# Weighing the six expert rows of a token on TensorE in pairs, with the rows of a pair stacked on the two partition halves

## The reference

```python
scores = jax.nn.sigmoid((x2 @ w_router).astype(jnp.float32))
_, idx = lax.top_k(scores + router_bias.astype(jnp.float32), TOP_K)     # TOP_K = 6
gate = jnp.take_along_axis(scores, idx, axis=1)
gate = gate / jnp.sum(gate, axis=-1, keepdims=True) * ROUTED_SCALE
...
yb = (jax.nn.silu(xb @ w_gate[eb]) * (xb @ w_up[eb])) @ w_down[eb]      # one block of an expert's tokens
acc = acc.at[tok_b].add(yb * gate_b[:, None])                            # six weighted rows per token
shared = (jax.nn.silu(x2 @ w_sh_gate) * (x2 @ w_sh_up)) @ w_sh_down
...
x = layer_norm(DEEPNORM_ALPHA * x + acc[:T] + shared, ln2_g[i], ln2_b[i])
```

## Time and profile before

| what | us |
|---|---|
| median of three runs | 2006.47 |
| the profiled execution's own time | 1997.47 |
| its span, first to last instruction | 1995.7 |
| busy: PE / DVE / ACT / POOL | 1804.0 / 800.1 / 381.5 / 375.5 |
| Combination of layer 0, first L974 to last L1026 | 900.48 to 951.74 |
| Combination of layer 1, first L974 to last L1026 | 1940.14 to 1991.40 |

### The profile page before, as it was taken

The page is one execution under the profiler, slowest core; times in us unless marked ns, Lnnn a source line. Parts: engine busy times, 40 slices in busy tenths (PEclk is TensorE's granted clock), DMA queues, the critical chain, the costliest instruction groups (busy, mean ns, idle before and its releaser), DMA issues. The chain is left out here.

```text
span 1995.7 us, 35283 instructions
## 1 busy us (share of the span) xinstructions
PE 1804.0 (90%) x12176; PEld 1112.1 (56%) x12177; DVE 800.1 (40%) x2156; ACT 381.5 (19%) x874; POOL 375.5 (19%) x499
## 2 busy tenths in 40 slices
PE   9999999889999989879899869999789999997787
PEld 7888445446666545544344428754456666664443
DVE  4222753623333222226276763415523333332236
ACT  2111741001111111101244533211001111110020
POOL 8452000011111111110013752200011111111110
PEclk9999999989999999999899968999899999999999
DMA  6220224599999999997122120107699999999987
GB/s 232 84 70 17 96 113 191 206 401 414 420 420 421 420 421 420 421 416 296 58 70 74 41 53 3 54 33 283 279 419 394 424 421 423 421 423 423 423 364 295
DMA packets 144053, 541.75 MB, mean 271 GB/s; under 512 B 30902, under 2 KB 68370, under 8 KB 94174
## 3 DMA queue, kind: packets, MB, share of 16 engines
q1 hardware_dynamic: 122654, 490.20, 61.3%
q0 software_dynamic: 21312, 50.37, 6.5%
HBM read 521.58 MB, written 46.14 MB: 284 GB/s over the span
## 5 line engine op out<-in xcount | busy, mean ns | idle before, releaser
L669 PE MATMUL bank<-W,XT 128*64 128x256 f32 x2880 | 335.5, 390 | 43.0 <-DMA W<-in_w_exp_gate_dram 15.8
L669 PEld LDWEIGHTS bank<-W,XT 128*64 128x64 f32 x2880 | 235.6, 141 | 154.7 <-issue 39.9
L704 PE MATMUL bank<-W,ht 128*64 128x512 f32 x720 | 168.0, 608 | 13.8 <-DMA W<-in_w_exp_down_dram 8.3
L2113 PE MATMUL bank<-XT,room 128*128 128x512 f32 x352 | 157.7, 603 | 0.0
L680 DVE TENSOR_TENSOR sig<-sig,bank 128x256 f32<-128x256 f32 x72 | 30.3, 421 | 274.7 <-ACT sig L676 264.4
L722 POOL DMA_INDIRECT y_rows<-y,row x36 | 36.7, 1020 | 430.6 <-DVE y L715 430.6
L682 DVE TENSOR_TENSOR h<-sig,bank 128x256 f32<-128x256 f32 x72 | 30.4, 422 | 209.9 <-PE bank L669 209.8
L2113 PEld LDWEIGHTS bank<-XT,room 128*128 128x128 f32 x352 | 66.8, 193 | 84.5 <-issue 84.1
L722 POOL DMA_INDIRECT y_rows<-XT,row x36 | 36.4, 1010 | 407.1 <-DVE XT L715 407.1
L655 ACT ACTIVATE XT<-bank 128x512 f32<-128x512 f32 x74 | 44.2, 597 | 330.5 <-PE bank L647 330.5
L669 PE MATMUL bank<-room,XT 128*64 128x256 f32 x864 | 98.7, 380 | 8.5 <-DMA room<-in_w_exp_gate_dram 8.0
(11 more groups left out here) (457 smaller groups left out, 2746.8 us busy)
## 6 DMA issues: line engine op xcount, KB each, us to landing
W<-in_w_exp_gate_dram SPq DMA_DIRECT2D x88, 1024.0 KB
W<-in_w_exp_up_dram SPq DMA_DIRECT2D x88, 1024.0 KB
W<-in_w_exp_down_dram SPq DMA_DIRECT2D x88, 1024.0 KB
room<-in_w_exp_gate_dram SPq DMA_DIRECT2D x40, 1024.0 KB
third_high<-in_w_exp_up_dram SPq DMA_DIRECT2D x40, 1024.0 KB
third_high<-in_w_exp_down_dram SPq DMA_DIRECT2D x40, 1024.0 KB
W<-y_rows SPq DMA_DIRECT2D x8, 2048.0 KB, 14.2
room<-in_rwkv_w_in_dram SPq DMA_DIRECT2D x22, 512.0 KB
```

The costliest lines, as they stand in the source:

```text
L669: last = pe.matmul((gate, up)[m][64 * a:64 * a + 64, :], xt[s][:, k, 64 * a:64 * a + 64], weights(w, a, m)[:, k * FE:(k + 1) * FE], start= ...
L704: last = pe.matmul(B[5 + half][64 * a:64 * a + 64, :], ht[:, j, 64 * a:64 * a + 64], weights(w, a, 2)[:, at:at + 512], start=(j == 0), sto ...
L2113: last = pe.matmul(main(i)[:], wc[i % WBUFS][:, kb, :], K.XT[:, kb, :], start=(kb == 0), stop=(kb == KD - 1))
```

## The change

All six rows of a token are weighed on PE, two by two. The two rows of a pair (row numbers 2q and 2q + 1) are loaded onto the two partition halves: row 2q of 64 tokens on partitions 0 to 63, row 2q + 1 of the same tokens on 64 to 127; the tile's other 64 tokens lie behind them on the same partitions (index h). The weight is 128 x 64: two diagonals of 64 x 64 on top of each other, with the gates of the two rows. One product with it gives the weighted sum of both rows for 64 tokens, and its result goes to output partitions 64h to 64h + 63.

For the diagonals the gates must lie on the halves in the same way; four small products with the identity put them there in the first pass of the expert loop, into bank 3, and ACT copies them out. The second pass's `turn_h`, which writes bank 3, waits for that copy. DVE loses L959. Per layer there are 24 DMAs of 512 KB instead of four of 2 MB and four of 1 MB, and each pair of rows has a semaphore of its own, for which PE waits.

```diff
-BY_VECTOR = 2
-BY_TENSOR = TOPK - BY_VECTOR
+ROW_PAIRS = TOPK // 2
+HP = P // 2
+BY_VECTOR = ()
+BY_TENSOR = [(t, q) for t in range(NT) for q in range(ROW_PAIRS) if (t, q) not in BY_VECTOR]
...
         def turn_h(pe, n):
             pe.wait_ge(hidden_done, n + 1)
+            if isinstance(n, int) and n == 1:
+                pe.wait_ge(ending.gates_kept, 1)
...
+        def turn_gates(pe):
+            for h in range(2):
+                for j in range(2):
+                    last = pe.matmul(gates_bank[HP * j:HP * j + HP, h], ident[:, HP * h:HP * h + HP],
+                                     K.gates[:, :, j:TOPK:2], start=True, stop=True)
+            last.then_inc(gates_turned, 1)
+
+        def keep_gates(act):
+            act.wait_ge(gates_turned, 1)
+            act.activation(turned_gates[:], gates_bank, ACT.Copy).then_inc(ending.gates_kept, 1)
...
                     if early and n == 0:
                         from_slot(0)
+                        turn_gates(pe)
...
                     keep_y(act, u, n, 0)
+                    if isinstance(n, int) and n == 0:
+                        keep_gates(act)
...
-        self.rows = K.arena.rearrange("p (t j d) -> p t j d", t=NT, j=TOPK)
+        self.rows = K.arena.rearrange("p (t q h d) -> p t q h d", t=NT, q=ROW_PAIRS, h=2)
         self.y = K.y_rows.rearrange("(j t p) d -> t p j d", j=TOPK, p=P)
-        self.diagonal = room[:, 0, :].rearrange("p (t j q) -> p t j q", t=NT, j=BY_TENSOR)
+        self.y_half = K.y_rows.rearrange("(j t h p) d -> t j p h d", j=TOPK, t=NT, h=2)
+        self.diagonal = room[:, 0, 0:2 * len(BY_TENSOR) * HP].rearrange("p (n h q) -> p n h q", h=2, q=HP)
+        self.two = room[:, 0, KD * FE - HP:KD * FE]
...
+    def load_pair(self, sp, t, q):
+        if (t, q) in BY_VECTOR:
+            sp.dma_start(self.rows[:, t, q], self.y[t][:, 2 * q:2 * q + 2]).then_inc(self.loaded[t][q], 16)
+            return
+        for j in range(2):
+            sp.dma_start(self.rows[HP * j:HP * j + HP, t, q], self.y_half[t][2 * q + j]).then_inc(self.loaded[t][q], 16)
...
         for t in range(NT):
-            sp.dma_start(self.rows[:, t, BY_VECTOR:TOPK], self.y[t][:, BY_VECTOR:TOPK]).then_inc(self.loaded_t[t], 16)
-            sp.dma_start(self.rows[:, t, 0:BY_VECTOR], self.y[t][:, 0:BY_VECTOR]).then_inc(self.loaded_v[t], 16)
+            for q in range(ROW_PAIRS):
+                self.load_pair(sp, t, q)
...
+    def row_product(self, pe, t, q):
+        B, n = self.K.banks, BY_TENSOR.index((t, q))
+        pe.wait_ge(self.diagonals, 2 * n + 2)
+        pe.wait_ge(self.loaded[t][q], 32)
+        for half in range(2):
+            for h in range(2):
+                last = pe.matmul(B[2 * t + half][HP * h:HP * h + HP, :], self.diagonal[:, n, h, :],
+                                 self.rows[:, t, q, h, half * 512:(half + 1) * 512],
+                                 start=False, stop=(q == ROW_PAIRS - 1))
+            if q == ROW_PAIRS - 1:
+                last.then_inc(self.summed, 1)
+
     def products(self, pe):
...
-        pe.wait_ge(self.diagonals, NT * BY_TENSOR)
         for t in range(NT):
-            pe.wait_ge(self.loaded_t[t], 16)
-            for half in range(2):
-                for j in range(BY_TENSOR):
-                    last = pe.matmul(B[2 * t + half][:], self.diagonal[:, t, j, :],
-                                     self.rows[:, t, BY_VECTOR + j, half * 512:(half + 1) * 512],
-                                     start=False, stop=(j == BY_TENSOR - 1))
-                last.then_inc(self.summed, 1)
-            if self.tiles is not None and t:
-                self.tiles.turn(pe, self.ln, t - 1)
+            for q in range(ROW_PAIRS):
+                self.row_product(pe, t, q)
+            if t:
+                self.turn(pe, t - 1)
+        self.turn(pe, NT - 1)
...
     def sums(self, dve):
...
         for t in range(NT):
-            dve.wait_ge(self.loaded_v[t], 16)
             dve.wait_ge(self.scaled, t + 1)
-            for j in range(BY_VECTOR):
-                step(dve.scalar_tensor_tensor(X[:, t, :], self.rows[:, t, j, :], K.gates[:, t, j:j + 1], X[:, t, :],
-                                              ALU.mult, ALU.add))
...
     def scale(self, act):
         K = self.K
-        for t in range(NT):
-            for j in range(BY_TENSOR):
-                act.activation(self.diagonal[:, t, j, :], K.ident[:], ACT.Copy,
-                               scale=K.gates[:, t, BY_VECTOR + j:BY_VECTOR + j + 1]).then_inc(self.diagonals, 1)
+        for j in range(2):
+            half = slice(HP * j, HP * j + HP)
+            act.activation(self.two[half, :], K.ident[half, half], ACT.Copy).then_inc(self.two_made, 1)
+        act.wait_ge(self.gates_kept, 1)
+        act.wait_ge(self.two_made, 2)
+        for n, (t, q) in enumerate(BY_TENSOR):
+            for h in range(2):
+                act.activation(self.diagonal[:, n, h, :], self.two, ACT.Copy,
+                               scale=self.gates[:, h, t, q:q + 1]).then_inc(self.diagonals, 1)
```

More of the change, by code:

```diff
@@ L558, in expert_loop @@
         y = [xt_room[:, 0:D], sb("y1", [P, D])[:]]
+        turned_gates = sb("turned_gates", [P, 2, NT, ROW_PAIRS])
         sig, h = sb("sig", [P, FE]), sb("h", [P, FE])
@@ L562, in expert_loop @@
         third = [[K.room[:, 0, :], K.room[:, 1, :]], [high[:, 0, :], high[:, 1, :]], [high[:, 2, :], high[:, 3, :]]]
-        ending = Combination(K, L, scope, shared, out, next_weights, high)
+        ending = Combination(K, L, scope, shared, out, next_weights, high, turned_gates)
         slots = B[4][:, 0:4]
+        gates_bank = B[3][:, 0:2 * NT * ROW_PAIRS].rearrange("p (h t q) -> p h t q", h=2, t=NT)
         gate, up = B[2][:, 0:FE], B[7][:, 0:FE]
@@ L574, in expert_loop @@
         stored = [sem("stored0"), sem("stored1")]
+        gates_turned = sem("gates_turned")
         steps = sem("steps")
@@ L882, with __init__ @@
 class Combination:
-    def __init__(self, K, L, scope, shared, out, next_weights, room):
+    def __init__(self, K, L, scope, shared, out, next_weights, room, turned_gates):
         def sem(name):
             return scope.sem(f"combine{L}_{name}")
-        self.K, self.shared, self.out, self.next_weights = K, shared, out, next_weights
-        self.rows = K.arena.rearrange("p (t j d) -> p t j d", t=NT, j=TOPK)
+        self.K, self.shared, self.out, self.next_weights, self.gates = K, shared, out, next_weights, turned_gates
+        self.rows = K.arena.rearrange("p (t q h d) -> p t q h d", t=NT, q=ROW_PAIRS, h=2)
         self.y = K.y_rows.rearrange("(j t p) d -> t p j d", j=TOPK, p=P)
-        self.diagonal = room[:, 0, :].rearrange("p (t j q) -> p t j q", t=NT, j=BY_TENSOR)
+        self.y_half = K.y_rows.rearrange("(j t h p) d -> t j p h d", j=TOPK, t=NT, h=2)
+        self.diagonal = room[:, 0, 0:2 * len(BY_TENSOR) * HP].rearrange("p (n h q) -> p n h q", h=2, q=HP)
+        self.two = room[:, 0, KD * FE - HP:KD * FE]
         self.down_room = room[:, 3, :]
[L895 to L898, removed]
+        self.loaded = [[sem(f"rows_{t}_{q}") for q in range(ROW_PAIRS)] for t in range(NT)]
+        self.added, self.two_made, self.diagonals, self.summed, self.scaled, self.gates_kept, self.y_stored = (
+            sem(n) for n in ("added", "two_made", "diagonals", "summed", "scaled", "gates_kept", "y_stored"))
         self.ln = LayerNorm(K, scope, f"ln2_{L}", K.in_["ln2_g"][L:L + 1, :], K.in_["ln2_b"][L:L + 1, :],
@@ L919, in load, with shared_product @@
             sp.wait_ge(K.out_stored, 16 * NT)
-    def products(self, pe):
-        B, shared = self.K.banks, self.shared
-        pe.wait_ge(shared.loaded, 16)
-        def shared_product(t):
-            for half in range(2):
-                for j in range(2):
-                    pe.matmul(B[2 * t + half][:], shared.hidden[:, j, t * P:(t + 1) * P], shared.w[:, j, half * 512:(half + 1) * 512],
-                              start=(j == 0), stop=False)
+    def shared_product(self, pe, t):
+        B, shared = self.K.banks, self.shared
+        for half in range(2):
+            for j in range(2):
+                pe.matmul(B[2 * t + half][:], shared.hidden[:, j, t * P:(t + 1) * P], shared.w[:, j, half * 512:(half + 1) * 512],
+                          start=(j == 0), stop=False)
+    def row_product(self, pe, t, q):
+        B, n = self.K.banks, BY_TENSOR.index((t, q))
+        pe.wait_ge(self.diagonals, 2 * n + 2)
+        pe.wait_ge(self.loaded[t][q], 32)
+        for half in range(2):
+            for h in range(2):
[4 more added lines that the diff above has]
+                last.then_inc(self.summed, 1)
+    def products(self, pe):
+        pe.wait_ge(self.shared.loaded, 16)
         for t in range(NT):
@@ L954, in sums @@
             dve.tensor_scalar_mul(X[:, t, :], X[:, t, :], ALPHA).then_inc(self.scaled, 1)
+        for t, q in BY_VECTOR:
+            dve.wait_ge(self.loaded[t][q], 16)
+            dve.wait_ge(self.scaled, t + 1)
+            for j in range(2):
```

(6 more changed lines are left out.)

6 lines of the change are left out of this document (3 added, 3 removed).

## The result

| | before | after |
|---|---|---|
| median of 4 runs each, us | 2005.76 (1999.50 to 2008.48) | 2056.62 (2050.71 to 2060.78) |
| the profiled execution, us | 1997.47 | 2050.71 |
| Combination of layer 0, from the first ALPHA times x to the end of the norm, us | 49.42 | 72.33 |
| Combination of layer 1, likewise | 49.42 | 70.78 |

A forecast was written before the change was run, and what follows sets the result against it. Weight stream bounds the expert loops, DVE the Combinations, after the change the load of the rows. Layer 0's +17.4 and layer 1's +17.0 on the profiled 1997.47 us gave 2031.9, plus 9.0 to the median 2041 us; range 2010 to 2060.

The forecast's parts named there:

- The load's rate: Load of the rows in both Combinations: 240 GB/s, 52.4 us a layer, with ends at 59.1 and 30.7 us.
- Landing and wait: End of each Combination's row load: 0.9 us until PE starts on the last pair, with 1 us more as other end.
- PE's last half: After the last pair lands: 4 PE instructions, 0.91 us, and the drain before DVE's first add, together about 1.3 us.
- the last paragraph of the sum: PE's last products in each Combination: at the lower clock 0.9 us longer per layer, +2 us in all.
- DVE's rest: Last tile of each Combination, first add to end of norm: 5.75 us in layer 0, 5.74 in layer 1.
- Edits costed at nothing: ACT's diagonals, at most 7.8 us, SP's 24 issues, 9 to 14 us, and PE's narrow products: all hidden, zero.
- gates in the loop: Four small products per layer in the expert loop's first pass, covered by the weight stream: zero, at most 2.4 us.
- 9.0 us up to the median: Whole kernel: the profiled execution before lay 9.0 us below the median of the runs; this was added unchanged.
- Rival 1: Row load in both Combinations keeps its full rate: 4.3 and 4.2 us less per layer, 1998 us; chance 0.18.
- 2: Row load: engines drift partly, 262 to 359 GB/s, 48.0 to 35.0 us, total 2032 down to 2006; chance 0.14.
- 4: Row load: each DMA costs a fixed piece, for example 0.5 us, 12 us a layer, 2022 us; chance 0.03.
- 3: PE's row products bound the Combinations at 0.43 us an instruction: +11 a layer, 2028 us at full load rate; chance 0.03.

The follow-up runs named there:

- the version with full rate: The changed kernel with y_rows stored in blocks of 64 tokens, so one 1 MB DMA brings a row pair to all 128 partitions: 2004.38 us, ratio to before 0.9997.

## Why the prediction came out as it did

It was right in sign, in mechanism and in range: the load of the rows ends last and flows at about half of its rate because each DMA writes one partition half, as the runs with all and with every other partition show. The size was 16 us short. Point by point:

- **The load's rate** is the term that was mis-sized. Forecast 240 GB/s, from the 1.5 us in which 192 KB go to each half; measured 220, so 57.2 us in place of 52.4, +4.8 us a layer. The window of 213 GB/s, of a load to one half, was nearer. What lifts the short one to 240 the traces don't tell; its share of 0.79 was a warning that it is no steady rate.
- **Landing and wait, 0.9 us**: the load ends by its rate at 966.1, PE starts at 967.07. Held.
- **PE's last half, 1.3 us**: 1.62 us from 967.07 to DVE's add at 968.69, because the clock was at its lower level, as the last paragraph of the sum had warned: 8 instructions take 3.22 us at a granted clock of 0.58 on average, after 2.68 us idle, against 1.94 at the full clock. A row pair at the full clock was priced at 1.82.
- **DVE's rest, 5.75 us**: 968.69 to 974.75, 6.06; the second add waits 0.22 us for PE. Together +0.6 us for both terms in layer 0.
- So layer 0's Combination ended 23.0 us later than before instead of 17.4, and layer 1's added 21.4 instead of 17.0.
- **Edits costed at nothing** (ACT's diagonals, SP's issues, the narrow products): nothing in the Combinations, as the 128-partition run shows. ACT needs 0.52 + 5.84 us, under the 7.8 allowed. The **gates in the loop** were given zero to 2.4 us; alone they cost 0.14%, 2.8 us, with none not excluded. Their cover was argued from the weight stream, and that holds for the work of PE, but not for what more code does to the stalls.
- **Between the Combinations** the forecast had nothing. The profiled execution has 8.8 us there: 6.9 up to the first scatter, where two executions of one kernel differ by 5.7 too, and 2.0 behind it. Own execution: 5.6 + 4.4 + 8.8 = 18.8 us over the forecast 2031.9, which is 2050.7.
- **9.0 us up to the median** was added unchanged. Before's profiled execution was a quick one: in its first stretch it lies 5.7 us under its second profile. The changed one's was not, and its median is only 5.9 above it, so the 18.8 us come down to 15.7 over the forecast. By medians the change costs 50.9 us; 44.3 of them, 22.9 + 21.4, are the Combinations, and the rest is the later stalls and scatter of the runs, which 4 runs don't part.
- By the 208 GB/s that the prediction estimates from the Trainium skill ("SBUF — State Buffer") it had 2057 us, and the median is 2056.6. That is closer than the rule earned: the load took 57.2 us and not 60.5, and the stretch between the Combinations, which the rule says nothing of, filled the difference.
- **Rivals**: 1, 2 and 4 fall with the 220 GB/s at a share of 1.03, 3 with products 0.24 us an instruction at the full clock. Rival 1's arithmetic held in the version with full rate (947.45 against 947.5), but the 1998 us that it gave did not: the kernels that bring the gain start layer 1's loop 5 to 9 us slower.

## What to carry to other kernels

Ask of each transfer which partitions one DMA writes, not only how many bytes: keep all 128, or every other one, within each DMA, for example by laying out the DRAM side so that one DMA fills both halves. Before a rate from a short window is used, look at the share beside it; of the three small windows here the slowest, 213 GB/s, was the nearest to the 220 of the long load. And when a stage becomes faster and the kernel doesn't, line up the stages of two profiles of each kernel: some of the difference repeats and some doesn't.

## What the runs showed of the hardware

- 64 partitions in one DMA: 206 to 222 GB/s where they lie in one half, 400 to 417 where they are every other one, both with the DMA engines full (1.02 to 1.05). The busy share alone doesn't show the loss.
- Two queues that write one half each reach 275 to 284 GB/s at the same share.
- SP's issues slow down behind a long queue: the 24 of layer 0 took 33.74 us, those of layer 1 began at 0.6 and became 2.0 us each or more. With all 128 partitions the last ones took mostly 1.05 to 1.2 us each, so the slower flow shows here too. Nothing waited for them.
- PE stalls of 3 to 5 us, once 9.45, by "issue" in the first passes of layer 1's loop, at a place that moves with the kernel, and only as long as 16 KB instruction transfers still come. The Trainium skill ("Runtime: NRT & Kernel Launch", "Instruction fetch mechanics") says that a branch to code outside the fetched pages stalls an engine. The times of the instruction transfers and the run with longer code fit that. That PE waits for these very transfers, and why a stall lasts three to five times as long as one of them, is not shown.
